# Residuals of six tiles in eight added by GpSimd's transfers in place of VectorE, squares one tile later

## What is computed

```
def rms_norm(x, g):
    y = x32 * lax.rsqrt(jnp.mean(x32 * x32, axis=-1, keepdims=True) + EPS)
    return (y * g).astype(x.dtype)

# block 1
mix = einsum('blc,cd->bld', concatenate([o, y]), w_out)
h_res = h_res + rms_norm(mix, post_mix_g)            # pass 0
h = rms_norm(h_res, pre_ffn_g)
f = silu(einsum('bld,df->blf', h, w_gate)) * einsum('bld,df->blf', h, w_up)
f = einsum('blf,fd->bld', f, w_down)
h_res = h_res + rms_norm(f, post_ffn_g)              # pass 1
# block 2, the same shape: mixer, then pass 2, feed-forward, then pass 3
```

## Time and profile before

| | us |
|---|---|
| median of 3 runs | 2554.29 |
| lowest, highest | 2551.48, 2565.74 |
| profiled execution, its own time | 2558.24 |
| span of the profiled execution | 2556.4 |
| TensorE busy | 2414.3 |
| VectorE busy | 1472.2 |
| GpSimd busy | 1154.2 |
| ScalarE busy | 799.4 |

### The profile page before, as it was taken

The page is one execution under the profiler, slowest core; times in us unless marked ns, Lnnn a source line. Parts: engine busy times, 40 slices in busy tenths (PEclk is TensorE's granted clock), DMA queues, the critical chain, the costliest instruction groups (busy, mean ns, idle before and its releaser), DMA issues.

```text
span 2556.4 us, 32817 instructions
## 1 busy us (share of the span) xinstructions
PE 2414.3 (94%) x11718; PEld 1957.8 (77%) x11718; DVE 1472.2 (58%) x2113; ACT 799.4 (31%) x1517; POOL 1154.2 (45%) x888
## 2 busy tenths in 40 slices
PE   8997888897999999999999998889989999999997
PEld 7976765675888888888778886778768888888885
DVE  5974776536556555555575202664645655556556
ACT  4231356524222222222241002552532222222222
POOL 3210040453655665555682533001745665556553
PEclk9998899899999999999999999999999999999999
DMA  5445520032111111111341212001311111111114
GB/s 146 128 130 131 174 76 1 9 107 91 46 54 56 55 49 49 49 49 49 105 149 58 55 44 107 1 1 42 130 44 52 59 50 49 49 49 49 50 57 152
DMA packets 176915, 179.29 MB, mean 70 GB/s; under 512 B 39704, under 2 KB 139544, under 8 KB 176816
## 3 DMA queue, kind: packets, MB, share of 16 engines
q1 hardware_dynamic: 171520, 164.02, 21.1%
q10 hardware_dynamic: 5296, 13.96, 1.6%
HBM read 147.46 MB, written 30.49 MB: 70 GB/s over the span
## 4 chain that ended last, share of the span: by engine, by line
PE 83%; DVE 8%; ACT 3%; issue 2%; POOL 2%; DMA 2%; SPq 0%; POOLq 0%; DVEq 0%; ACTq 0%
PE ps L267 23%; PE ps L269 23%; PE ps L268 23%; PE ps L1466 3%; PE ps L1498 3%; PE ps L1484 2%; PE ps L474 1%; DVE hbuf L425 1%; ACT ex L1552 1%; DVE hbuf L2019 1%; PE ps L2741 1%; DVE ex L1583 0%; PE ps L456 0%; DMA msb<-ssm_lags 0%; DVE hbuf L431 0%
## 5 line engine op out<-in xcount | busy, mean ns | idle before, releaser
L2019 DVE TENSOR_TENSOR hbuf<-hbuf,ps 128x1024 f32<-128x1024 f32 x320 | 390.7, 1221 | 245.5 <-PE ps L269 223.6
L267 PE MATMUL ps<-mlp_dh,mlp_fh 128*128 128x512 f32 x672 | 263.8, 393 | 4.7 <-DVE hbuf L2019 4.4
L269 PE MATMUL ps<-mlp_dh,mlp_fl 128*128 128x512 f32 x672 | 263.0, 391 | 0.0
L268 PE MATMUL ps<-mlp_dl,mlp_fh 128*128 128x512 f32 x672 | 262.3, 390 | 0.0
L207 POOL TENSOR_TENSOR wgt<-raw,ones 128x512 fp32r<-128x512 f32 x76 | 87.2, 1148 | 324.5 <-PE ps L269 165.9
L1785 POOL TENSOR_TENSOR mlp_s_raw<-mlp_gh_raw,mlp_s_raw 128x512 f32<-128x512 f32 x44 | 57.1, 1297 | 284.1 <-PE ps L269 284.1
L267 PEld LDWEIGHTS ps<-mlp_dh,mlp_fh 128*128 128x128 f32 x672 | 126.3, 188 | 35.6 <-DVE hbuf L2019 8.1
L269 PEld LDWEIGHTS ps<-mlp_dh,mlp_fl 128*128 128x128 f32 x672 | 126.3, 188 | 27.5
L268 PEld LDWEIGHTS ps<-mlp_dl,mlp_fh 128*128 128x128 f32 x672 | 126.3, 188 | 27.3
L1798 POOL TENSOR_TENSOR mlp_dl<-mlp_d_raw,mlp_dh 128x1024 fp32r<-128x1024 f32 x42 | 113.9, 2711 | 46.5 <-ACT mlp_dh L1997 46.5
L2056 DVE TENSOR_TENSOR mlp_fl<-mlp_p,mlp_fh 128x512 fp32r<-128x512 f32 x42 | 114.4, 2725 | 3.6
(11 more groups left out here) (485 smaller groups left out, 6699.7 us busy)
## 6 DMA issues: line engine op xcount, KB each, us to landing
h<-hbuf SPq DMA_DIRECT2D x24, 512.0 KB, 2.9
mlp_d_raw<-in_w_down SPq DMA_DIRECT2D x21, 512.0 KB, 3.5
mlp_d_raw<-in_w_ffn_out SPq DMA_DIRECT2D x21, 512.0 KB, 3.7
raw<-in_w_in SPq DMA_DIRECT2D x40, 256.0 KB, 2.7
raw<-in_w_out SPq DMA_DIRECT2D x32, 256.0 KB, 2.6
res_b<-h SPq DMA_DIRECT2D x16, 512.0 KB, 4.3
mlp_ul<-in_w_up SPq DMA_DIRECT2D x22, 256.0 KB, 3.0
mlp_uh_raw<-in_w_up SPq DMA_DIRECT2D x22, 256.0 KB, 3.3
```

Of the source, the lines that this page charges most:

```text
L267: pe.matmul(out, lhs[0], rhs[0], start=first, stop=False, skip_group_check=over)
L268: pe.matmul(out, lhs[0], rhs[1], start=False, stop=False, skip_group_check=over)
L269: return pe.matmul(out, lhs[1], rhs[0], start=False, stop=last, skip_group_check=over)
L2019: v.tensor_tensor(self.acc[:, i, :], self.acc[:, i, :], src, ALU.add).then_inc(self.s["added"], 1)
```

## The change

For the tiles 0 to 5 of each pass (`N_ADD` = 6) the residual is no longer loaded into `res` and added by VectorE. GpSimd issues a transfer from DRAM onto the normed tile in `hbuf` that adds (`pool_res`, accum_op=ALU.add). It waits for the norm of the tile and for the landing of the transfer two tiles before; its own landing takes the place of the signal `h` for the store and the second square (`whole`). Tiles 6 and 7 stay with SP and VectorE; their loads are issued up front. Second squares and second roots run one tile later, in passes 0 and 2 ahead of the first square and first root of the round. Three semaphores of small loads in the first stage are merged into others, so that three waits there now wait for more loads.

```diff
+            self.res_added = [sem(f"post_res_added{j}") for j in range(2)]
         def sp_res(self, sp, i):
-            if i == 0 and stored[0]:
+            if i == N_ADD and stored[0]:
                 sp.wait_ge(sem("stored"), stored[0])
+            sp.dma_start(self.res[:, i % 2, :], rows(self.res_dram, i)).then_inc(self.res_in[i % 2], 16)
+
+        def whole(self, eng, i):
+
+            if i < N_ADD:
+                eng.wait_ge(self.res_added[i % 2], 16 * (self.n * N_ADD // 2 + i // 2 + 1))
+            else:
+                eng.wait_ge(self.h, self.n * (NT - N_ADD) + i - N_ADD + 1)
+
+        def pool_res(self, pool, i):
+            if i == 0 and self.n:
+                pool.wait_ge(sem("stored"), 16 * NT * self.n)
             if i >= 2:
-                sp.wait_ge(self.h, self.tiles(i - 1))
-            sp.dma_start(self.res[:, i % 2, :], rows(self.res_dram, i)).then_inc(self.res_in[i % 2], 16)
+                self.whole(pool, i - 2)
+            pool.wait_ge(self.normed, self.tiles(i + 1))
+            pool.dma_start(self.m[:, i, :], rows(self.res_dram, i), accum_op=ALU.add)\
+                .then_inc(self.res_added[i % 2], 16)
 
         def sp_store(self, sp, i):
-            sp.wait_ge(self.h, self.tiles(i + 1))
+            self.whole(sp, i)
...
         def act_sq2(self, act, i):
-            act.wait_ge(self.h, self.tiles(i + 1))
+            self.whole(act, i)
...
         def dve_res(self, v, i):
-            v.wait_ge(self.res_in[i % 2], 16 * (self.tiles(i) // 2 + 1))
+            if i < N_ADD:
+                return
+            v.wait_ge(self.res_in[i % 2], 16 * (self.n * (NT - N_ADD) // 2 + (i - N_ADD) // 2 + 1))
...
+    N_ADD = 6
...
-        load(sp, "maskf", xf[:, :], io["c_mask"])
+        load(sp, "lam", xf[:, :], io["c_mask"])
...
-            load(sp, "ssm_d", ddT[:, :], io["d_skip"][0].rearrange("(g h) -> h g", h=HG))
+            load(sp, "ssm_dt", ddT[:, :], io["d_skip"][0].rearrange("(g h) -> h g", h=HG))
...
             if first:
-                sp.wait_ge(self.turns.h, self.turns.tiles(NT))
+                for i in (NT - 4, NT - 3, NT - 2, NT - 1):
+                    self.turns.whole(sp, i)
...
@@ passes 0 and 2, ScalarE @@
             if i < NT:
                 empty(i)
+            if 0 <= i - 2 < NT:
+                post[n].act_sq2(act, i - 2)
+            if i < NT:
                 step = base + NT + i
                 act.wait_ge(emptied[step % 2], step // 2 + 1)
                 post[n].act_sq(act, i)
             if 0 <= i - 3 < NT:
                 post[n].act_hi(act, i - 3)
-            if 0 <= i - 1 < NT:
-                post[n].act_sq2(act, i - 1)
@@ passes 0 and 2, GpSimd @@
-        for i in range(NT + 1):
+        for i in range(NT + 2):
+            if i >= 2:
+                post[n].pool_root2(pool, i - 2)
             if i < NT:
                 post[n].pool_root1(pool, i)
-            if i >= 1:
-                post[n].pool_root2(pool, i - 1)
+            if 0 <= i - 1 < N_ADD:
+                post[n].pool_res(pool, i - 1)
@@ passes 0 and 2, SP @@
-        for i in range(2):
+        for i in range(N_ADD, NT):
             post[n].sp_res(sp, i)
...
         for i in range(NT):
             post[n].sp_store(sp, i)
-            if i + 2 < NT:
-                post[n].sp_res(sp, i + 2)
@@ pass 1, GpSimd @@
-        for i in range(NT + 2):
+        for i in range(NT + 3):
             for k in range((2, 1, 1)[i] if i < 3 else 0):
                 pool_weights(pool, u, u + 1)
                 u += 1
             if i < NT:
                 post[1].pool_root1(pool, i)
-            if i >= 2:
-                post[1].pool_root2(pool, i - 2)
+            if i >= 3:
+                post[1].pool_root2(pool, i - 3)
+            if 0 <= i - 2 < N_ADD:
+                post[1].pool_res(pool, i - 2)
@@ pass 3, GpSimd @@
         for i in range(NT):
             post[3].pool_root1(pool, i)
+            if 0 <= i - 1 < N_ADD:
+                post[3].pool_res(pool, i - 1)
@@ pass 1, ScalarE @@
-            if 0 <= i - 2 < NT:
-                post[1].act_sq2(act, i - 2)
+            if 0 <= i - 3 < NT:
+                post[1].act_sq2(act, i - 3)
@@ first stage, VectorE @@
-        loaded(v, "maskf")
+        loaded(v, "lam", 5)
         v.tensor_copy(maskb[:, :], xf[:, :])
-        loaded(v, "lam", 4)
+        loaded(v, "lam", 5)
```

More of the change, by code:

```diff
@@ L1061, in dve_ssm_params @@
     def dve_ssm_params(v, link):
-        loaded(v, "ssm_dt")
+        loaded(v, "ssm_dt", 2)
         exact_exp(v, link, pv("edt"), pv("dt"), pv("k"), pv("r"))
@@ L1128, in dve_ssm_params @@
             c, s = f"c{n}", f"s{n}"
-        loaded(v, "ssm_d")
+        loaded(v, "ssm_dt", 2)
         link(v.tensor_tensor(dsk[:, :, :], bc(ddT[:, :], 2, HG), bc(ident[0:HG, 0:HG], 1, GR), ALU.mult))
@@ L2603, in _ @@
             post[1].sp_store(sp, i)
-            if i + 2 < NT:
-                post[1].sp_res(sp, i + 2)
             if i < NRAW:
@@ L2623, in _ @@
             post[3].sp_store(sp, i)
-            if i + 2 < NT:
-                post[3].sp_res(sp, i + 2)
         sp.wait_ge(sem("stored"), stored[0])
```

## The result

The changed kernel takes 2613.0 us (median; 2611.7 to 2615.1), the kernel before 2555.2 on the same chip. The ratio is 1.0212, with a 95% interval from 1.0191 to 1.0234 (it is estimated from all the runs; the two medians alone would give 1.0226): slower, by 2.1%, and whether by more or less than 2% the interval leaves open. The prediction said 2587.6 us, in a range from 2556 to 2618: the direction came as forecast, and so did the closed loop of passes 0 to 2; the size is 25 us beyond the likeliest value, and the gain forecast for the tail did not come. The profiled execution has a span of 2609.8 us, 53.4 more than before.

A forecast was written before the change was run, and what follows sets the result against it. TensorE, busy 94%, was taken as the bound, VectorE in the tail. Delays of 12.1, 15.3 and 7.9 us in passes 0, 2 and 1, less 2.0 in the tail, add 33.3 to 2554.3: 2587.6 us, range 2556 to 2618.

The forecast's parts named there:

- the closed loop of passes 0 to 2: Passes 0 to 2: each landing gates the next transfer; landings 8.9 us apart in passes 0 and 2, 7.7 in pass 1.
- the gain forecast for the tail: Pass 3: fewer VectorE additions bring the last accumulation 5.6 us sooner; with DMA engines as cover, -2.0 us taken.
- A: Passes 0 to 2: the adding transfer's landing, 4.6 to 7 us, paces three passes; 2568 to 2617 us; chance 0.60.
- B: Short landing, 3.5 to 4.6 us: loops keep TensorE's 6.45 us step, tail and passes cancel; say 2560 us; chance 0.20.
- C: Landing gates nothing, VectorE's additions were the bound: 13.9 us won, 2540 us; needs landing at most 3.1 us; chance 0.07.
- D: Issue stretched beside VectorE, or additions far under half rate: landing over 7 us, beyond 2618, say 2630 us; chance 0.13.
- three signs of being wrong: Landings at the step's own 6.5 us; a tail that doesn't shorten; additions holding the DMA engines no longer than a copy.
- The landing: Adding transfer, GpSimd's issue to landing: 3.5 load + 1.5 second read + 0.5 issuing = 5.5 us, between 3.5 and 7.0.
- The term, 7.9: Pass 1: late start and loop delay the fifth step of the next projection, through root, scaling and turn, by 7.9 us.
- a over 7.3: Pass 3: GpSimd waits for landing i-2, so issue-to-landing time over 7.3 us (twice 3.66) would alone eat the gain.
- The saving on VectorE: All passes: six of eight residual additions per pass go, 24 x 1.23 = 30 us of VectorE.
- The edits costed at nothing: First stage: mask copy and parameters wait for up to four more small loads, landed 17 us before; no cost.

## Why the prediction was right, and by how much it missed

**Which rival.** The forecast, A, holds. B's short landing (under 4.6 us) is what the plain transfer has, 3.9, and the adding one does not. C falls: ScalarE waits for each of the 18 landings of passes 0 to 2. D needed a landing over 7 us; only the tail has that, 8.2. Of the three signs of being wrong that the prediction named, one came: a tail that doesn't shorten.

**The landing.** 5.5 was taken, 5.6 measured. Its parts were 3.5 for the load, 1.5 for the second read and 0.5 for issuing. With the add taken away 3.9 are left, and the engines are held 1.5 us less; this confirms the second read, while no run parts the other two. The Trainium skill ("Collectives: The Full Stack", "The bandwidth ceiling: the fold count and why AG ≠ RS ≠ AR") states for ReduceScatter that the add pays for two source reads, which makes it half as fast as the copies of AllGather; the local transfers of this case agree with it, 3.15 us against 1.61. By the formula of the Trainium skill in "DMA: Bandwidth & Descriptors", "Anatomy of one DMA — SWDGE (gpsimd) path", the estimate was 3.2 us and with that a faster kernel; the measured 5.6, and even the plain transfer's 3.9, are longer.

**The loop of passes 0 and 2.** Forecast 8.9 us a turn, measured 9.67 and 9.63. The term that was too small is the 2.11 us from a square to the end of its root, taken from the earlier trace rows, where the small addition ran unstretched. In the changed kernel the second root releases a scaling on VectorE just before, and the addition takes 1.03 us in place of 0.22. Over six turns this is 4.6 us; pass 2 missed by 3.6 (18.9 for 15.3), pass 0, whose delay was counted down to one wait of TensorE, by 1.5 (13.6 for 12.1). In the two other traces of the same passes the misses are 2.1 and 4.4 in pass 0 and 8.2 and 4.8 in pass 2 at the same pace of the loop, so the split is no finer than that; that pass 0 came so near its forecast is partly luck.

**Pass 1.** The loop's pace was right: 7.7 forecast, 7.6 measured. The term, 7.9, should have been 15.4. What failed here is the path from the landing to TensorE: the prediction followed root, scaling and turn alone. It named who waits for the landing, and of those the second square; it did not go through what is queued behind that square on ScalarE, which from the eighth round on is the gelu. That is 5.2 us by the run with the gelu first. TensorE's waits grew by 12.5 us in all (16.1 for 3.6). The remaining 2.3 us are of the size of the matmuls at half clock behind the waits, for which the prediction put nothing, and of the scatter; no run parts them.

**Pass 3.** Forecast -2.0, measured +2.4. The accumulations came ahead by 6.2 us, 5.6 forecast (the squares, which follow them, lie 18.0 us apart from first to last, not 24.2). The loads on the DMA engines were priced rightly, 17.8 us for six additions (50.9% of a window of 35 us, 2.97 each) against 3.1 each. The step that failed is the end: the prediction took full engines up to the end of the span as its bound (+0.6) and put the gain at 2.0 us, but it is the order that decides. Crowded additions land after 8.2 us at the median, GpSimd waits for landing i-2 and so issues the last one only at 2595.51, and three stores wait in SyncE's queue for its landing at 2604.2. While they wait the engines run dry (busy share 0.08 from 2604 to 2605). VectorE's own work ended 2.8 us sooner than before, and the span 5.1 us later after it. The prediction had GpSimd's wait as a bound ("a over 7.3") and did not apply it to a landing stretched by the stores. Half-size transfers turn the same tail into -5.4 us.

**The rest.** 3.4 us between passes 1 and 2 go with a lower clock there, of the change or of the single execution; the traces don't part the two. The saving on VectorE, 30 us in the prediction, was 20.5; none of the terms uses it. The edits costed at nothing show nothing: the span before pass 0 moved by -0.2 us.

## What to carry to other kernels

When an operation leaves an engine for a transfer, write down the closed loop that its landing enters, and then go along each in-order engine that waits for the landing and name everything queued behind the wait: here they are the gelu (5.2 us), GpSimd's small addition (0.8 us a turn in two passes) and SyncE's stores in the tail (4.4 us off the forecast). A loop of one transfer per tile costs its latency each time; issue the transfer so that its landing has two rounds, and put the waiting operation behind as little as possible. The engine that is relieved must be the bound for the relief to show: of the four passes only the tail had it, and there the stores that stood behind the last landing took it back.

## What the runs showed of the hardware

- An adding transfer into SBUF of 512 KB, issued by GpSimd, lands after 5.6 us and holds the 16 DMA engines 3.15 us; written over instead of added, 3.9 and 1.61 us; 256 KB added, 4.2 and 1.72 us. In the crowded tail the median of the first is 8.2 us.
- GpSimd is occupied 0.94 us by issuing an adding transfer, whole or half a tile, and 0.63 by a plain one.
- An addition of one column on GpSimd took 0.22 us alone and 1.03 to 1.32 us beside a two-input operation of VectorE over 1024 columns.
- A norm on VectorE (128x1024) took 1.28 us, and 4.55 beside GpSimd's issue of a transfer and two of its splits of weights.
- The granted clock of one stretch (0.81 or 1.00 over 25 us) differed between executions whose pass 1 was the same, and went with 2.5 us more in the stage; that of a window of 10 us behind pass 0 was 1.00 or 0.83 in two executions of the same pass.
